# Second attention: the scaling of the probabilities moved from VectorE to ScalarE, its reciprocal by Ln and Exp

## The reference

```python
def moba_attention(q, k, v):      # 8 heads of 64, one block of 256 keys
    ...
    l_own = (jnp.einsum("bhqd,bhkd->bhqk", qc, k_own) * scale - slopes * dist_own)
    l_own = jnp.where(dist_own >= 0, l_own, -jnp.inf)
    ...
        p_own = jax.nn.softmax(l_own, axis=-1).astype(v.dtype)
        o = jnp.einsum("bhqk,bhkd->bhqd", p_own, v_own)

def mixer_ab(h, w_in, conv_w, ln_g, ln_b, w_out):
    u = h @ w_in
    ...
    return jnp.concatenate([ya, yb], axis=-1) @ w_out     # ya: convolution branch, yb: attention
```

## Time and profile before

| | us |
|---|---|
| median of 3 runs | 911.66 |
| lowest, highest | 910.96, 911.79 |
| the profiled execution | 911.4 |
| its span, first to last instruction | 909.7 |
| TensorE busy | 875.7 |
| VectorE busy | 615.6 |
| ScalarE busy | 467.9 |

### The profile page before, as it was taken

How to read it: one execution, slowest core, us unless ns; L and a number is a source line. 1 busy time by engine, 2 the same in 40 slices (tenths; PEclk the granted TensorE clock), 3 DMA queues, 4 the chain that set the end, 5 groups by cost and what they waited for, 6 DMA issues and landing times.

```text
span 909.7 us, 19313 instructions
## 1 busy us (share of the span) xinstructions
PE 875.7 (96%) x7294; PEld 841.6 (93%) x7294; DVE 615.6 (68%) x988; ACT 467.9 (51%) x751; POOL 101.0 (11%) x140
## 2 busy tenths in 40 slices
PE   8999999999999989998999999999998999999996
PEld 7988899999999979777899999999898899999996
DVE  5676567665665687867766666668879966666665
ACT  6546765443443484446644444445776644444443
POOL 3320002000000049210100000002140100000000
PEclk9999999999999999999999999999999999999999
DMA  7432246556556548424365555554435355555551
GB/s 265 164 117 93 94 162 221 180 177 201 180 173 206 179 149 238 136 77 156 122 203 189 184 186 185 184 185 140 162 115 187 130 195 184 184 186 185 185 182 47
DMA packets 44434, 152.10 MB, mean 167 GB/s; under 512 B 5604, under 2 KB 6884, under 8 KB 44388
## 3 DMA queue, kind: packets, MB, share of 16 engines
q1 hardware_dynamic: 41184, 145.52, 48.8%
q0 software_dynamic: 2400, 4.89, 1.7%
q10 hardware_dynamic: 804, 1.04, 0.3%
HBM read 148.64 MB, written 1.05 MB: 165 GB/s over the span
## 4 chain that ended last, share of the span: by engine, by line
PE 85%; DVE 10%; ACT 3%; issue 1%; DMA 1%; SPq 0%; DVEq 0%; POOL 0%; ACTq 0%
PE bank L1302 26%; PE bank L1304 26%; PE bank L1303 26%; DVE alo L918 4%; DVE wlo L893 2%; PE bank L1653 1%; DVE h L928 1%; ACT whi L505 1%; PE bank L1742 1%; DMA raw<-in_slabs 1%; PE bank L1409 1%; DVE proj L937 1%; PE bank L1432 1%; PE bank L1336 1%; DVE sq L1235 1%
## 5 line engine op out<-in xcount | busy, mean ns | idle before, releaser
L1302 PE MATMUL bank<-ahi,whi 128*128 128x256 f32 (+1 forms) x1400 | 401.5, 287 | 6.5 <-DVE alo L912 3.4
L1304 PE MATMUL bank<-ahi,wlo 128*128 128x256 f32 (+1 forms) x1400 | 394.1, 281 | 0.0
L1303 PE MATMUL bank<-alo,whi 128*128 128x256 f32 (+1 forms) x1400 | 393.8, 281 | 0.0
L893 DVE TENSOR_TENSOR wlo<-raw,whi 128x1024 fp32r<-128x1024 f32 x273 | 332.2, 1225 | 33.8 <-ACT whi L505 33.5
L505 ACT ACTIVATE whi<-raw 128x1024 fp32r<-128x1024 f32 x273 | 282.3, 1050 | 112.0 <-PE bank L1304 97.3
L1302 PEld LDWEIGHTS bank<-ahi,whi 128*128 128x128 f32 x1400 | 264.5, 189 | 11.7 <-DVE alo L912 3.9
L1303 PEld LDWEIGHTS bank<-alo,whi 128*128 128x128 f32 x1400 | 264.6, 189 | 0.5
L1304 PEld LDWEIGHTS bank<-ahi,wlo 128*128 128x128 f32 x1400 | 264.6, 189 | 0.0
L1302 PE MATMUL bank<-hidhi,whi 128*128 128x256 f32 x704 | 197.6, 281 | 3.2 <-issue 2.1
L1303 PE MATMUL bank<-hidlo,whi 128*128 128x256 f32 x704 | 196.9, 280 | 0.0
L1304 PE MATMUL bank<-hidhi,wlo 128*128 128x256 f32 x704 | 196.9, 280 | 0.0
(11 more groups left out here) (220 smaller groups left out, 702.9 us busy)
## 6 DMA issues: line engine op xcount, KB each, us to landing
raw<-in_slabs SPq DMA_DIRECT2D x273, 512.0 KB, 3.5
shared<-in_convw POOLq DMA_DIRECT2D x4, 512.0 KB, 7.0
shared<-zpad POOLq DMA_DIRECT2D x48, 35.5 KB, 3.2
raw<-in_slabs SPq DMA_DIRECT2D x8, 128.0 KB, 5.6
vtok<-in_gatew POOLq DMA_DIRECT2D x2, 512.0 KB, 3.9
out<-y SPq DMA_DIRECT2D x4, 256.0 KB, 2.7
h<-in_xT ACTq DMA_DIRECT2D x3, 272.0 KB, 5.6
h<-in_xT SPq DMA_DIRECT2D x1, 272.0 KB, 3.5
```

The lines of the kernel that those rows point to most:

```text
L893: dve.tensor_tensor(wlo[:, n % R, :, :], raw[:, n % R, :, :], whi[:, n % R, :, :].bitcast(F32), ALU.subtract).then_inc(lo_done, 1)
L1302: pe.matmul(dst, hi, xh, start=start, stop=False, skip_group_check=True)
L1303: pe.matmul(dst, hi, xl, start=False, stop=False, skip_group_check=True)
L1304: return pe.matmul(dst, lo, xh, start=False, stop=stop, skip_group_check=True)
```

## The change

In the second attention ACT does the step `normalized` itself: the natural logarithm of the two sums, the exponential of its negative (which is the reciprocal), and the two multiplications as copies with a factor for each partition. It stands at the head of the odd slots 1 to 15, ahead of the split. DVE keeps the step in the first attention only (`s0 == 0`). What waits for `p_normed` stays as it was.

```diff
@@ scalar engine
+            def normalized(s, s0, keys):
+
+                n, u = keys[s % 2], 2 * s
+                act.wait_ge(p_ready, 2 * (s0 + s) + 2)
+                link(act.activation(rinv[:, u:u + 2], rsum[:, u:u + 2], ACT.Ln))
+                link(act.activation(rinv[:, u:u + 2], rinv[:, u:u + 2], ACT.Exp, scale=-1.0))
+                for hd in range(2):
+                    pr = prob[:, 2 * (s % 2) + hd, 0:n]
+                    act.activation(pr, pr, ACT.Copy, scale=rinv[:, u + hd:u + hd + 1]).then_inc(p_normed, 1)
...
             for u in range(MOBA_U + 3):
+                if u % 2 and u < MOBA_U:
+                    normalized(u // 2, FOX_S, MOBA_N)
                 if u in IN2_STEP or u in OUT2_STEP:
                     split_ahead(n)
                     n += 1
@@ vector engine, softmax_slot
                     if u % 2 == 0:
                         maxima(u // 2, s0, keys, biased)
-                    else:
+                    elif s0 == 0:
                         normalized(u // 2, s0, keys)
```

## The result

| | us |
|---|---|
| before, median of 13 runs on one chip | 911.01 |
| changed, median of 13 runs on the same chip | 913.86 (912.04 to 915.49) |
| ratio, 95% interval | 1.0033 (1.0024 to 1.0043) |
| the profiled execution, its span | 913.85, 912.1 |

By the ratio the change costs 3.0 us (2.2 to 3.9), by the medians 2.85. All of the interval lies above 1.002, the edge up to which the prediction said "same" (0.51); so the kernel is slower, to which it had given 0.43.

A forecast was written before the change was run, and what follows sets the result against it. TensorE, busy 96% of the span, was taken as the bound, through its waits between 360 and 430 us. Terms 0.65 - 0.73 + 1.20 + 0.64 gave +1.76 us on the median 911.66: 913.4, range 912.0 to 914.6.

The forecast's parts named there:

- same: Verdict that the time stays within about 0.2% (1.8 us), reaching to 913.48 us; chance 0.51.
- The reading of what bounds the kernel: Whole kernel: TensorE, busy 96% of the span, sets the end; only its waits between 360 and 430 us matter.
- The prices: Second attention: a step costs ACT 1.08 or 1.28 us; ACT gains about 9.4 us, DVE loses about 6.7.
- the lower bound: Price of a scaling on ACT as cheap as the Squares without a column: 0.33 and 0.22 us start to start.
- Slots 1 to 7 hidden: Softmax steps 0 to 3: splits start up to 1.3 us later, but TensorE reads them later; cost 0.
- slot 9 at +0.65: Softmax step 4: TensorE's 2.20 us wait for the probabilities grows, and it goes on 0.65 us late.
- given back in slots 10 to 13: DVE's chain loses step 5's 0.73 us, so it stands at -0.08 and output row 0 moves by 0.1 only.
- Steps 6 and 7, +1.12 and +0.64: Slots 13 to 17: whi and row 1 are 1.12 us late, then 0.64 more by output row 3.
- rival B: Row 1: longer idle time brings 1.2 GHz instead of 2.4; +0.6 us beyond the sum, +0.8 with longer column, 914.2; chance 0.21.
- the sum: Second attention: 0.65, less 0.73 on DVE, plus 1.20, plus 0.64 give +1.76 us; 912.7 to 914 has chance 0.55.
- Rival C: Output rows held by DVE, not ACT; two steps of about 0.73 us leave the chain: -1.5, 910.2; chance 0.06.
- Rival A: Cheap pieces give +1.30 us; a later column under less half clock behind slot 10 gives +1.0, 912.7; chance 0.18.

The follow-up runs named there:

- steps_0_5: ACT makes only softmax steps 0 to 5, DVE keeps 6 and 7; against the kernel before, ratio 0.9999 (0.9990 to 1.0008).
- fill_row1_again: The whole change plus 14 zero-adding matmuls in TensorE's wait before row 1, rerun beside whole_change; 912.97 us, ratio 1.0025 to the kernel before.
- whole_change: The changed kernel itself, timed again in another session; 914.31 us, ratio 1.0039 (1.0026 to 1.0053) to the kernel before.
- steps_6_7: ACT makes only softmax steps 6 and 7, DVE keeps the others; against the kernel before, ratio 1.0020 (1.0011 to 1.0029).
- recip_on_dve: The whole change, but DVE takes the reciprocals again and ACT only scales; 912.04 us, ratio 1.0014 (1.0005 to 1.0024) to the kernel before.
- fill_slot10: The kernel before plus 16 matmuls into a free PSUM bank in TensorE's wait of slot 10; 910.05 us, ratio 0.9990 to the kernel before.

## Why the prediction was right, and where it was not

**The reading of what bounds the kernel** held. TensorE's waits between 360 and 430 us set the loss; the busy shares of ACT (52% now) and DVE did not.

**The prices** held. Ln took 0.195 us and Exp 0.203 (0.21 foretold), 0.22 to 0.23 from start to start, the two scalings of 128 columns 0.69 together and those of 256 columns 0.91, the sum of a step 1.07 and 1.28. ACT gained 9.5 us (9.4). VectorE gave up 5.9 us, not 6.7: the prediction added whole lengths of neighbours that overlap (two scalings of 0.35 and a reciprocal of 0.16 in 0.73). The row with a column operand, L523, was the right neighbour, and the lower bound was not needed. The rule of the Trainium skill ("ScalarE: Activation LUTs", section "Rules for kernel authors") that a multiplication belongs to VectorE was not what decided. The prices agree with it: a scaling took 0.28 to 0.35 us on VectorE and 0.39 to 0.50 on ACT. (The 1.28 us that the prediction set beside it as the trace's was its own sum for a whole step, with Ln and Exp.) But the same work on ACT costs nothing over steps 0 to 5 and gains 3 us in slot 8.

**Slots 1 to 7 hidden, slot 9 at +0.65, given back in slots 10 to 13:** right, +0.57 measured at the transposes, and steps_0_5 shows the whole of it at 0.9999. Its parts are a loss and a gain that cancel: +0.57 in slot 10, and less work for VectorE in slot 11. The wait before row 1 became 2.11 us, not the foretold 1.9, though row 1 came when it should: TensorE had less to wait for in front of row 0 and reached the transposes of step 6 0.08 us early (418.86 - 419.23 + 0.29), where the prediction had row 0 0.1 late.

**Steps 6 and 7, +1.12 and +0.64:** right. +1.11 was measured at the split of slot 13, and fill_row1_again, where the wait before row 1 is filled and its clock stays up, leaves 1.70 us at row 3 against 1.76.

**The step that failed is the clock, rival B.** The half clock in row 1 was given a chance of 0.21 and kept out of the sum. It came in all three profiled executions with a wait of 2.1 us there (the change, whole_change, steps_6_7). Its size was near the upper end of what rival B said or above it: +0.6 to 0.8 foretold, 0.8 at row 3 of the change and 1.0 between whole_change and fill_row1_again. With 0.8 on top, the sum is 2.56 and the measured row 3 is 2.57 late. The reasoning took the length of the last idle time as the thing that decides, 1.9 us against 0.92 and 2.20. The traces contradict that from both sides: the clock fell behind 1.54 us (recip_on_dve, row 1), held behind 2.36 (recip_on_dve, slot 10), and went both ways behind 2.11 and 2.12 in one and the same program. What does decide, no run here shows.

The sum was also a sum for one execution, while the result is taken over many whose clocks differ.

**Rival C**, DVE as the holder of the output rows, has no part: DVE's wait for the whi of slot 13 grew with the change (2.11 us, 0.27 before).

**Rival A** said that a column that starts later runs less under the half clock behind slot 10. It did not: 16 matmuls ran under it before and 16 after. That this stretch costs something holds: with the wait filled, fill_slot10 is 1.46 us earlier at row 3, and 0.9 by the ratio.

What stays open: the profiles say where the clock fell in one execution of each kernel; of the others only its mean over the execution is on record. The 13 runs of the change spread over 3.5 us (912.04 to 915.49), those of the kernel before over 2.1 (909.65 to 911.79, without the one of 1591.85). The profiled executions show what the mean says: one stretch at half clock, not counting the last microseconds of the kernel, goes with 0.996, two with 0.994 to 0.995, three with 0.993 and four with 0.991. The 13 runs of the change have 0.989 to 0.993. By an estimate from these figures each of them had three or more such stretches; where, is not known.

## What to carry to other kernels

Work moved to the idler engine is free or dear by what stands behind it in that engine's queue: here the same step gained 3.1 us in a slot where ACT was waiting anyway, cost nothing over six places taken together (one of them lost 0.6 us, and the relief of the old engine gave it back), and cost 1.1 us where the next instruction was the split that the output row was waiting for. Before a step is moved, look for the place where the new engine idles and the consumer waits, and put it there, ahead of the instruction that waits.

A wait that looks harmless because it only grows by a microsecond can bring a stretch at half clock with it. Here it came behind waits of 1.54 to 2.83 us, sometimes and not always. Where a change lengthens such a wait in front of a dense stretch, put the half clock into the sum with its chance, and try a filler of useless matmuls to see what it is worth. Compare many executions of each kernel before a trace of one is taken for all.

## What was not expected of the hardware

- Useless work made the kernel faster: 14 matmuls in row 1's wait saved 1.3 us between the medians, 16 in slot 10's wait 1.3 between the medians and 0.9 by the ratio.
- The length of an idle time did not by itself tell whether the clock fell: it fell to 0.50 behind 1.54 us and stayed at 1.00 behind 2.36 in the same execution, and behind 2.11 and 2.12 us in one program it did one in one execution and the other in another.
- A stretch at half clock can be free: near 640 us it shortened the wait that followed from 1.82 to 0.56 us.
- A table load on ACT (1.28 us) is followed by the next instruction within 0.02 us (427.63 + 1.28 against 428.93), and Ln and Exp after each other have none between them.
